# Attention outputs with V stationary, in two float32r parts and channel-major, normalised through DRAM

## What is computed

```python
h = rmsnorm(x); qa, ka, va, qf, kf, vf, gate = split(h @ w_in)   # 8 + 8 heads of 64 channels
# heads 0..7: softmax over keys t-s in three dilated windows, ALiBi bias, mixed by their denominators
# heads 8..15: s = q.k/8 + (c[t] - c[s]), causal, c = cumsum(log_sigmoid(gate + b_forget))
p = softmax(s);  y_head = p @ v_head
x = x + concat(y) @ w_out
```

## Time and profile before

| | us |
|---|---|
| median of three runs | 1726.58 |
| the profiled execution: span, first to last instruction | 1724.9 |
| TensorE busy | 1672.5 (97%) |
| VectorE busy | 729.9 (42%) |
| ScalarE busy | 586.3 (34%) |
| GpSimd busy | 0.2 |

### The profile page before, as it was taken

How to read it: one execution, slowest core, us unless ns; L and a number is a source line. 1 busy time by engine, 2 the same in 40 slices (tenths; PEclk the granted TensorE clock), 3 DMA queues, 4 the chain that set the end, 5 groups by cost and what they waited for, 6 DMA issues and landing times.

```text
span 1724.9 us, 22386 instructions
## 1 busy us (share of the span) xinstructions
PE 1672.5 (97%) x8592; PEld 1417.7 (82%) x8592; DVE 729.9 (42%) x1371; ACT 586.3 (34%) x1014; POOL 0.2 (0%) x4
## 2 busy tenths in 40 slices
PE   5999999999999799999999999999999999999997
PEld 4788888888888688898888888888888888888886
DVE  6444444444444544652343364342424242424235
ACT  5445545445455542430252242121313130303022
POOL 0000000000000000000000000000000000000000
PEclk9999999999999899999999999999999999999999
DMA  5001110011010331251102012120202020203012
GB/s 187 17 25 27 38 27 16 24 40 27 25 39 13 112 109 37 69 151 49 37 25 74 16 34 62 58 77 13 85 12 85 12 85 12 85 3 94 0 37 97
DMA packets 99972, 87.72 MB, mean 51 GB/s; under 512 B 3984, under 2 KB 87056, under 8 KB 99888
## 3 DMA queue, kind: packets, MB, share of 16 engines
q1 hardware_dynamic: 99904, 86.75, 16.3%
HBM read 82.41 MB, written 4.85 MB: 51 GB/s over the span
## 4 chain that ended last, share of the span: by engine, by line
PE 89%; DVE 4%; ACT 4%; issue 1%; DMA 1%; SPq 0%; DVEq 0%
PE psG L527 18%; PE psG L529 18%; PE psG L528 18%; PE psG L544 15%; PE psO L676 7%; PE psS L625 3%; PE psG L607 2%; PE psS L556 2%; PE psS L555 2%; PE psS L811 1%; PE psS L572 1%; ACT khh L930 1%; PE psG L831 1%; DVE act_lo L1141 1%; DVE w_lo L1141 1%
## 5 line engine op out<-in xcount | busy, mean ns | idle before, releaser
L527 PE MATMUL psG<-act_hi,w_hi 128*128 128x512 f32 x640 | 249.5, 390 | 0.0
L529 PE MATMUL psG<-act_hi,w_lo 128*128 128x512 f32 x640 | 249.0, 389 | 0.0
L528 PE MATMUL psG<-act_lo,w_hi 128*128 128x512 f32 x640 | 249.0, 389 | 0.0
L527 PE MATMUL psG<-w_hi,a_hi 128*128 128x512 f32 x512 | 200.1, 391 | 0.7
L528 PE MATMUL psG<-w_lo,a_hi 128*128 128x512 f32 x512 | 199.3, 389 | 0.0
L529 PE MATMUL psG<-w_hi,a_lo 128*128 128x512 f32 x512 | 199.2, 389 | 0.0
L1110 ACT ACTIVATE r_ff<-psG 128x512 f32<-128x512 f32 x64 | 38.3, 598 | 446.7 <-PE psG L529 446.7
L1141 DVE TENSOR_TENSOR w_lo<-raw,w_hi 128x1024 fp32r<-128x1024 f32 x126 | 154.0, 1224 | 64.7 <-ACT w_hi L965 41.4
L1477 DVE TENSOR_TENSOR X<-X,psG 128x512 f32<-128x512 f32 x128 | 87.9, 687 | 212.9 <-PE psG L529 212.9
L676 PEld LDWEIGHTS psO<-V,pT 128*128 128x128 f32 x1152 | 149.8, 195 | 18.5 <-ACT pT L978 6.4
L965 ACT ACTIVATE w_hi<-raw 128x1024 fp32r<-128x1024 f32 x104 | 108.7, 1049 | 140.2 <-PE psG L529 83.0
(11 more groups left out here) (148 smaller groups left out, 2396.7 us busy)
## 6 DMA issues: line engine op xcount, KB each, us to landing
raw<-in_w_up_dram SPq DMA_DIRECT2D x32, 512.0 KB, 4.0
raw<-in_w_down_dram SPq DMA_DIRECT2D x32, 512.0 KB, 3.3
raw<-in_w_in_dram SPq DMA_DIRECT2D x22, 512.0 KB, 4.0
X<-in_x_dram SPq DMA_DIRECT2D x8, 512.0 KB, 8.2
raw<-in_w_out_dram SPq DMA_DIRECT2D x8, 512.0 KB, 3.9
raw<-in_w_xk_dram SPq DMA_DIRECT2D x8, 512.0 KB, 3.7
raw<-in_w_xv_dram SPq DMA_DIRECT2D x8, 512.0 KB, 3.7
raw<-in_w_xq_dram SPq DMA_DIRECT2D x8, 512.0 KB, 3.7
```

What stands on the lines that cost most here:

```text
L527: nc.tensor.matmul(dst, sh, mh, start=(k == 0), stop=False)
L528: nc.tensor.matmul(dst, sh, ml, start=False, stop=False)
L529: mm = nc.tensor.matmul(dst, sl, mh, start=False, stop=(k == n - 1))
```

## The change

The probabilities are now the moving operand. V is stored as high and low part side by side (128 columns for one head) and is stationary; the transposed probabilities, as high part `pT_hi` and low part `pT_lo`, stream 256 wide, two query blocks at once. Channels 0 to 63 of the result are V's high part, 64 to 127 its low part; ACT copies the lower half out, DVE adds it to the upper. The steps are reordered so that two query blocks of one head follow each other (`Q_TILES`), and the outputs (PV) come once in two steps, behind the transposes of a later step. The outputs are channel-major and not normalised: GpSimd stores each to a DRAM tensor `y_rows`. The row sums of a pair are collected in one tile, transposed once (RT), inverted and stored to `inv_rows`. In the last pair and after it SP loads a pair's outputs and its inverse sums (broadcast over the channels of a head), GpSimd multiplies them, and ACT and DVE split the result. X is not used as storage for outputs; its eight tiles are loaded again after the last pair, in SP's queue behind the last outputs. Four more tiles of the output product start in psS before the last pair's outputs are there.

```diff
-KEY_BLOCKS = (1, 2, 3, 8, 1, 8, 2, 7, 4, 7, 3, 6, 4, 6, 5, 5)
-S_BLOCKS = 11
+Q_TILES = ((0, 0), (1, 0), (0, 3), (0, 1), (1, 3), (1, 1), (0, 2), (1, 2))
+STEP = tuple((h, 2 * i + odd) for h, i in Q_TILES for odd in range(2))
+KEY_BLOCKS = tuple(qb + 1 for _, qb in STEP)
+S_BLOCKS = 15
+PT_SIZE = tuple(4 * i + 3 for _, i in Q_TILES)
@@ gaps
-        first = 1.0 + 0.15 * n
-        room += [first, max(0.2, 2.3 + 0.18 * n1 - 0.07 * n - first)]
+        scores = 0.24 * (1 + (n1 > 4)) + 0.11 * n1
+        outputs = 0.12 * 2 * PT_SIZE[u // 2 - 1] / 2 if u % 2 == 0 and u else 0.0
+        room.append(max(0.3, 1.1 + 0.3 * n - outputs) + max(0.0, 0.3 + 0.11 * n1 - scores))
@@ pair_steps
+        if u == STEPS - 1:
+            order.append(("RT", 0))
+        if u and u % 2 == 0:
+            order.append(("PV", u // 2 - 1))
...
+        if u == STEPS - 1:
+            order.append(("PV", N_Q_TILES - 1))
-Y_STEPS = (1, 2, 3, 4, 5, 6, 7, 8)
-EARLY_PRODUCTS = 2 * Y_PRODUCTS - 4
-VT_STEPS = (8, 10)
+Y_STEPS = (2, 3, 4, 5, 6, 7, 8)
+EARLY_PRODUCTS = 2 * Y_PRODUCTS
+VT_STEPS = (6, 10)
-        SPLIT_AT = {("T", 2): 1, ("PV", 6): 2, ("PV", 13): 3}
+        SPLIT_AT = {("T", 1): 1, ("T", 6): 2, ("T", 14): 3}
@@ SP
+            def y_load(k):
+                i = k % 2
+                sp.wait_ge(y_stored, 16 * N_Q_TILES * (k + 1))
+                sp.wait_ge(inv_stored, 16 * (k + 1))
...
+                if k >= 2:
+                    sp.wait_ge(y_lo, k - 1)
+                sp.dma_start(y_raw[i][:], y_rows[k]).then_inc(y_loaded[i], 16)
+                for h in range(2):
+                    inv = inv_rows[k, h * TT:(h + 1) * TT, :].rearrange("(a q) n -> a (q n)", a=1)
+                    sp.dma_start(y_inv[i][h * HEAD:(h + 1) * HEAD, :], inv.to_broadcast([HEAD, T])).then_inc(y_loaded[i], 16)
...
+            y_load(PAIRS - 1)
+            for t in range(TT):
+                if t == 0:
+                    sp.wait_ge(pv_done, PAIRS * N_Q_TILES)
+                sp.dma_start(X[:, t, :], x_t[t]).then_inc(x_loaded[t], 16)
@@ GpSimd, pair_pool
+                    if kind == "PV":
+                        pool.wait_ge(o_out, p * N_Q_TILES + (u + 1))
+                        pool.dma_start(rows.rearrange("o d n -> (o d) n"), y_out[u % 2][:]).then_inc(y_stored, 16)
+                        pool.wait_ge(y_stored, p * (16 * N_Q_TILES) + 16 * (u + 1))
+                        pool.sem_inc(y_free, 1)
+                    elif kind == "Y":
+                        y_scale(u)
+            def y_scale(k):
+                pool.wait_ge(y_loaded[k % 2], 48 * (k // 2 + 1))
+                nc.gpsimd.tensor_tensor(y_raw[k % 2][:], y_raw[k % 2][:], y_inv[k % 2][:], ALU.mult).then_inc(y_scaled, 1)
@@ TensorE
                     elif kind == "QK":
                         if u >= 2:
-                            pe.wait_ge(pT_done, p * 16 + (u - 1))
+                            pe.wait_ge(pT_lo_done, p * 16 + (u - 1))
@@ PV
-                        for b in range(qb + 1):
-                            mm = nc.tensor.matmul(psO[:, u % 2, 0:HEAD], pT[:, b * P:(b + 1) * P],
-                                                  V[par][:, b, h * HEAD:(h + 1) * HEAD], start=(b == 0), stop=(b == qb))
+                        for b in range(2 * i + 2):
+                            n = 1 if b == 2 * i + 1 else 2
+                            places = slice(first + 2 * b, first + 2 * b + n)
+                            for part in (pT_hi, pT_lo):
+                                mm = nc.tensor.matmul(psO[:, u % 2, 0:n * P], V[par][:, b, h, :],
+                                                      part[:, places, :].rearrange("p b n -> p (b n)"),
+                                                      start=(b == 0 and part is pT_hi), stop=(n == 1 and part is pT_lo))
@@ after the pairs
+            pe.wait_ge(inv_done, PAIRS)
+            for t in (2, 3, 4, 5):
+                early_products(t, 0, Y_PRODUCTS)
+            pe.wait_ge(y_lo, PAIRS)
@@ ScalarE
+            def y_hi_out(k):
+                act.wait_ge(y_scaled, k + 1)
+                nc.scalar.activation(act_hi[:, k, :], y_raw[k % 2][:], ACT.Copy).then_inc(y_hi, 1)
...
+                    elif kind == "VT":
+                        v_hi(u, 1 - par, 0, p * 2 + (u + 3))
+                    elif kind == "PV":
+                        act.wait_ge(pv_done, p * N_Q_TILES + (u + 1))
+                        nc.scalar.activation(o_low[:], psO[HEAD:P, u % 2, 0:2 * P], ACT.Copy).then_inc(o_low_out, 1)
@@ VectorE
                     elif kind == "PV":
+                        dve.wait_ge(o_low_out, p * N_Q_TILES + (u + 1))
+                        dve.wait_ge(y_free, p * N_Q_TILES + (u + 1))
+                        for odd in range(2):
...
+                            e = nc.vector.tensor_tensor(y_out[u % 2][:, odd * P:(odd + 1) * P], psO[0:HEAD, u % 2, at_],
+                                                        o_low[:, at_], ALU.add)
+                    elif kind == "T":
+                        n = KEY_BLOCKS[u]
+                        dve.wait_ge(pT_hi_done, p * 16 + (u + 1))
+                        lo_part(pt_places(pT_lo, u), psS[u % 2][:, 0:n * P].rearrange("p (b n) -> p b n", n=P),
+                                pt_places(pT_hi, u), pT_lo_done)
```

More of the change, by code:

```diff
@@ L59, with pt_start @@
 PRODUCTS = 3 * KT
-KEY_BLOCKS = (1, 2, 3, 8, 1, 8, 2, 7, 4, 7, 3, 6, 4, 6, 5, 5)
-STEP = tuple((KEY_BLOCKS[:u].count(n), n - 1) for u, n in enumerate(KEY_BLOCKS))
-S_BLOCKS = 11
+Q_TILES = ((0, 0), (1, 0), (0, 3), (0, 1), (1, 3), (1, 1), (0, 2), (1, 2))
+N_Q_TILES = len(Q_TILES)
+STEP = tuple((h, 2 * i + odd) for h, i in Q_TILES for odd in range(2))
+KEY_BLOCKS = tuple(qb + 1 for _, qb in STEP)
+S_BLOCKS = 15
+PT_BLOCKS = 22
+PT_SIZE = tuple(4 * i + 3 for _, i in Q_TILES)
+def pt_start(j):
+    return 0 if j % 2 == 0 else PT_BLOCKS - PT_SIZE[j]
 def gaps():
@@ L261, in hybrid_layer @@
         x_loaded = [sem(f"x_loaded{i}") for i in range(TT)]
-        x_rest = [sem(f"x_rest{i}") for i in range(2)]
         m_loaded = [sem(f"m_loaded{i}") for i in range(MT)]
@@ L319, in hybrid_layer, with pt_places @@
         B_TILES = PRO_TILES + 7 * len(PAIR_TILES)
+        def pt_places(part, u):
+            first, n, even = pt_start(u // 2), KEY_BLOCKS[u], 1 - u % 2
+            return part[:, first + even:first + even + 2 * n - 1:2, :]
         def S_of(u):
@@ L1321, in add_residual @@
                 cs = slice(half * HALF, (half + 1) * HALF)
-                nc.vector.tensor_tensor(X[:, t, cs], X[:, t, cs], psG[g % 2][:], ALU.add).then_inc(tile_out, 1)
-            for e in (2 * TT, 2 * TT + 1):
-                y_split(e)
+                src = out_bank(t) if g < G_OUT + TT else psG[g % 2][:]
+                nc.vector.tensor_tensor(X[:, t, cs], X[:, t, cs], src, ALU.add).then_inc(tile_out, 1)
+            y_split(PAIRS - 1)
             for t in range(1, TT):
```

270 lines of the change are left out of this document (142 added, 128 removed).

## The result

The changed kernel takes 1782.7 us (median of four runs, 1778.2 to 1784.1) against 1726.5: 1.0322 times as long, 95% interval 1.0308 to 1.0337. The forecast was 1746.4 with a range of 1700 to 1784: the direction held, the size did not (+56 us where +20 were forecast), and the range held by 1.3 us.

A forecast was written before the change was run, and what follows sets the result against it. TensorE's work was taken to bound seven pairs, the chain of waits the last. 1724.9 + 1.0 + 1.4 + 19.5 - 2.1 = 1744.7, and 1.7 gives 1746.4 us; range 1700 to 1784, the sum's own 1722 to 1780.

The forecast's parts named there:

- the seven steady pairs: Pairs with projections left: TensorE's saving is handed to waits, 68.0 us a pair, +1.4 us over seven.
- the last pair: Pair without projections: ScalarE and VectorE stand still for store, load and GpSimd's multiplication; 87.3 us against 67.5, +19.5 us.
- rival 2: Steady pairs, steps 14 to 3: TensorE's clock falls in the waits, 4 to 8 us a pair, 1775 to 1802; chance 0.12.
- The outputs on TensorE: Output matmuls in every pair: float32r 256 wide every 0.12 us; TensorE's work falls from 67.8 to 59.8 us, 8.0 a pair.
- Rival 3: Output matmuls: 256 columns in float32r with alternating halves take 0.23 us, as 512 do; 1771 us; chance 0.04.
- The waits in the steady pairs: TensorE waits for VectorE's low part or V around projection tiles' exits, listed by step; 8.4 us a pair.
- Rival 1: Steady pairs: TensorE stays the bound, waits shorter than listed; 1689 us with none, 1717 with half; chance 0.24.
- Behind it: Output product after the last pair: 150 products instead of 154, no transposes of X; 36.5 to 34.4 us, -2.1.
- start: Start of the kernel: two V copies go to ScalarE before the low part can start, +1.0 us.

The follow-up runs named there:

- e11: e8's kernel with the projection products of a steady pair reordered (14 in step 9, fourth tile ending in step 11); 1725.3 us, ratio 0.9992.
- e13: The changed kernel with e11's order of the projection products and no other edit; 1760.1 us, ratio 1.0201.
- e4: The changed kernel with ScalarE and VectorE taking each output of the last pair two steps later, GpSimd's order unchanged; 1762.1 us, ratio 1.0203.
- e7: The changed kernel with the mask load ahead of the Q load, steady-pair projection products set by hand, and e4's edit; 1737.7 us, ratio 1.0063.
- e8: e7's kernel with the last pair's 42 early products spread over steps 5 to 11 instead of 9 to 15; 1736.0 us, ratio 1.0059.
- e2: The changed kernel without VectorE's low pass of the probabilities, TensorE streaming the high part twice; 1757.9 us, ratio 1.0181.
- e6: The changed kernel with 124 extra matmuls, results unread, in the last pair where TensorE waits; 1778.5 us, ratio 1.0295.
- e9: e8's kernel with steady-pair products moved again and the first four X loads ahead of the last pair's output load; 1759.7 us, ratio 1.0181.

## Why the prediction was right in direction and short in size

**The steps that failed.** The forecast gave the seven steady pairs +1.4 us and they took +23.3; it gave the last pair +19.5 and it took +31.2. In the first term the mask load's place in SyncE's queue was missing (11 us), the clock was taken as full (some 14 us), and TensorE's own gain was put too high (another 14); the waits were put too high and the pairs of the kernel before too short, which hid 17 us of that. In the second the mechanism was right and the chain of passes too short. The sum's own range, 1722 to 1780, was missed. That the time still lay under 1784 was luck: this end of the range was put there for rival 2, whose clock was to cost 4 us a pair or more.

**The outputs on TensorE: rate right, gain mis-sized.** In the changed kernel the 256-wide matmuls follow each other in 0.12 us:

```profile
440.24 0.38 PE L759 MATMUL psO<-pT_hi,V 128*128 128x256 f32 x1 [1.22 <-DVE pT_lo L1228]
440.46 0.28 PE L759 MATMUL psO<-pT_lo,V 128*128 128x256 f32 x1
440.58 0.28 PE L759 MATMUL psO<-pT_hi,V 128*128 128x256 f32 x1
```

Rival 3 is out. But a pair's TensorE busy time fell from 67.49 to 62.40 us at full clock, 5.1 and not 8.0. Summed from each instruction's start to the next one's, the outputs went from 14.9 to 9.7 us (forecast 15.3 to 8.6: the eight-block group of the earlier trace rows is a little dearer a block than the mean, and the first of a group takes 0.22), the projections with their returns from 36.2 to 35.5 (forecast 1.4 less), and the scores behind a wait 0.6 more.

**The waits in the steady pairs: places right, sum a little high.** The list by hand gave 2.1 us before step 3's scores (2.1 measured), 1.8 for V's low part before step 8's (1.5) and 1.2 before the last outputs (1.2). In all 8.4 a pair, measured 6.4 in the pair shown and 6.8 on the mean. The claim behind it, that what TensorE saves is handed to waits, held for this order of products; e11 and e13 show that it is the order's doing and no property of the two passes. Rival 1 (half of the waits, 1717 us) was therefore not wrong about the engines' room, only about this order.

**The mask: the step that was missing.** I had costed the split that moves by its own duration and not by what SyncE has queued behind the load that waits for it. That is 11 us of waiting, of the 21.9 by which the steady pairs missed.

**The clock: rival 2, in small.** The seven steady pairs have granted clocks of 0.95 to 1.00, and their busy time is 446.9 us where e11, at 1.00 in all seven, has 432.3 for the same matmuls: some 14 us. Rival 2 wanted 4 to 8 us a pair in steps 0 to 3 and got 2 on the mean. It came with the waits: in e11, where no wait but the one that opens the first pair (2.1 us) is over 1.4 us, the same stretches run at 1.00. The rule of the Trainium skill (TensorE: Matmul & The Clock Gate, "A second HAM failure mode") agrees in kind, since waits of TensorE were followed by the lower level; the price it had here is these 14 us.

**The base.** Three of the seven pairs of the kernel before last 69.7 to 70.3 us. The first has three waits of 0.7 to 1.4 us at its start; the others have one wait each, of 2.1 us in the pair from 216.84 to 286.83 and of 1.7 two pairs later:

```profile
PE psS L555 <- issue: 2.1, 1, 2.1
```

The forecast took the earlier trace rows's 67.8 for all. The changed kernel's lists have no such wait. These 6.3 us (480.9 less 7 x 67.8) go the other way, and together (work +14, clock +14, mask +11, other waits -11, base -6.3, on a forecast of +1.4) they are the 23.3 to within a microsecond.

**The last pair: mechanism right, chain too short.** The multiplication took 2.34 us (2.4 forecast; the Trainium skill's page, GPSIMD Engine Reference, section 3.1, gave the estimate of 2.25, and the trace agrees), the store 2.1 to 3.8 from its issue to the multiplication behind it (2.4). From the scores of step 1 to the end of y_split(0) took 19.2 us (17.6), from there to y_split(6) 51.1 (46.4), the steps behind 26.7 (23.3); and these scores began 2.7 us behind the pair's first maximum where it had been 1.0, behind the previous pair's last outputs, which the forecast did not have. The terms that were too small: the low pass beside the multiplication (three times 1.05 us), and the passes of the last seven steps. Without the stand-still (e4) the pair still takes 10 us more than before; the place of the early products accounts for 1.7 of them (e7 to e8), and leaving the low pass of the probabilities out gave 2.9 us, in e2, with the stand-still in place. The clock (0.74 there, 0.86 in the kernel before) was tried with the stand-still alone (e6). The rest may be the additional pass and copy in each step's chain; that was argued and not tried, and it stays open.

**Behind it.** Forecast -2.1, measured +2.5: the X loads, now queued behind the last output load, land last, and TensorE waits 2.3 us at the half's turn (0.8 in e6, for a reason that no run shows). The prediction named this and priced it at 0. Bringing four of them forward (e9) delayed the output load instead.

**The sum.** 36.3 us were missing: steady pairs 21.9, last pair 11.7, behind it 4.6, start -0.5, and -1.4 because the forecast added 1.7 for the median over the traced span, where it was 0.3.

## What to carry to other kernels

When a step is moved, go down every queue that waits for it and ask what stands behind the waiting entry: here 14 us hung on two DMA issues in the wrong order. When a change lightens the bounding engine under a fixed order of work, the gain comes back only after the filler work is set anew, and its order has to be judged twice, as cover for a step's chain and by where its own results leave. And a result that takes a round trip should be asked for some steps after it is begun, not in the step that begins it.

## What the runs showed of the hardware

- GpSimd's multiplication of 128x1024 float32 took 2.34 us, a VectorE pass of that shape with both inputs in SBUF 1.22. Beside each other they took turns, whichever began first. All 26 such passes (act_lo or w_lo, over all the traces) that began while a multiplication ran ended 1.08 to 1.09 us behind its end: 2.28 us for act_lo at 603.59, 2.72 for w_lo in e4 at 638.22, where the multiplication had begun at 637.50. Six times the pass began first; it kept its 1.22 or 1.23, and the multiplication took 2.81 to 3.21 us. In e4:

```profile
616.15 1.23 DVE L1230 TENSOR_TENSOR act_lo<-y_raw,act_hi 128x1024 fp32r<-128x1024 f32 x1 [2.11 <-ACT act_hi L1052]
616.46 3.12 POOL L601 TENSOR_TENSOR y_raw<-y_raw,y_inv 128x1024 f32<-128x1024 f32 x1 [1.44 <-DMA y_inv<-inv_rows]
```

  The maximum at 599.17 in e4, from PSUM and SBUF, kept its 1.23 beside the one of 597.12, which took 2.37. The Trainium skill (GPSIMD Engine Reference, section 1, Specifications) says that GpSimd's SBUF interfaces are shared with VectorE and that they collide for VectorE instructions with two SBUF inputs; the trace agrees. The price is no fixed one: it is what is left of the instruction that began first.
- A reciprocal of 16x128 out of PSUM took 0.95 us, as long as a low pass over six blocks.
- In the changed kernel's steady pairs the granted clock fell to its lower level seven times, each time during a wait of 1.5 to 5.5 us or at most 1.5 us behind it (in e8 behind one of 2.2 us, then a stretch at 0.50). Such a wait did not always bring it: the pair of 294.47 read 1.00 with one of 2.1 us, and e11 read 1.00 for all seven pairs with one of 2.1 us in the first.
